# A fused two-layer block on one core: 64 instead of 48 tokens take their expert up rows by gather, and the tensor engine's up rounds are written out

## What is computed

```
q = (xt @ w_query).reshape(T, PEER_HEADS, 2, PEER_HALF)
scores = einsum('thpc,hpnc->thpn', q, sub_keys);  top 16 of each half, top 16 of the 256 sums
experts = i1 * 128 + i2            # 8 heads x 16 = 128 experts of 16384 for each token
u = take(expert_down, experts);    hdn = gelu(einsum('ted,td->te', u, x))
vsel = take(expert_up, experts);   y = einsum('te,ted->td', gates * hdn, vsel)
```

## Time and profile before

| | us |
|---|---|
| median of 3 runs (3017.72 to 3021.58) | 3018.91 |
| the profiled execution, its own time | 3036.75 |
| its span, first to last instruction | 3034.7 |
| PE busy in the span | 2999.1 (99%) |
| DVE busy | 1970.3 (65%) |
| ACT busy | 1473.1 (49%) |
| POOL busy | 945.9 (31%) |

### The profile page before, as it was taken

The page is one execution under the profiler, slowest core; times in us unless marked ns, Lnnn a source line. Parts: engine busy times, 40 slices in busy tenths (PEclk is TensorE's granted clock), DMA queues, the critical chain, the costliest instruction groups (busy, mean ns, idle before and its releaser), DMA issues.

```text
span 3034.7 us, 44598 instructions
## 1 busy us (share of the span) xinstructions
PE 2999.1 (99%) x16703; PEld 2676.0 (88%) x16703; DVE 1970.3 (65%) x2549; ACT 1473.1 (49%) x1794; POOL 945.9 (31%) x675
## 2 busy tenths in 40 slices
PE   9999999999999999999999999999999999999998
PEld 8999888888888888998999999999878888888887
DVE  5445564688875555687988976645776555555554
ACT  6445454555564444544444444554555434444443
POOL 3110000088888887155777840000000000000000
PEclk9999999999999999999999999999999999999999
DMA  7764467577777778898999985654446666666664
GB/s 228 246 205 140 147 216 253 187 210 204 213 204 203 225 209 260 296 334 308 351 363 351 349 308 193 191 180 136 132 146 187 192 191 193 191 191 193 190 193 153
DMA packets 227280, 672.30 MB, mean 222 GB/s; under 512 B 57116, under 2 KB 60838, under 8 KB 226737
## 3 DMA queue, kind: packets, MB, share of 16 engines
q1 hardware_dynamic: 157696, 549.79, 55.5%
q0 software_dynamic: 63680, 103.36, 11.8%
q10 hardware_dynamic: 5744, 16.99, 1.5%
HBM read 631.85 MB, written 38.12 MB: 221 GB/s over the span
## 4 chain that ended last, share of the span: by engine, by line
PE 95%; DVE 2%; issue 1%; ACT 1%; DMA 1%; ACTq 0%; SPq 0%; DVEq 0%
PE ps L1954 14%; PE ps L2248 10%; PE ps L2095 8%; PE ps L2097 8%; PE ps L2096 8%; PE ps L1933 8%; PE ps L1934 8%; PE ps L1932 8%; PE ps L1953 7%; PE ps L2247 5%; PE ps L1950 1%; PE ps L2261 1%; PE ps L2260 1%; PE ps L2262 1%; DVE w_lo L691 1%
## 5 line engine op out<-in xcount | busy, mean ns | idle before, releaser
L691 DVE TENSOR_TENSOR w_lo<-raw,w_hi 128x1024 fp32r<-128x1024 f32 (+2 forms) x1072 | 1274.0, 1194 | 855.7 <-ACT w_hi L686 801.1
L686 ACT ACTIVATE w_hi<-raw 128x1024 fp32r<-128x1024 f32 (+2 forms) x1072 | 1107.4, 1034 | 1274.0 <-PE ps L1934 338.4
L1954 PE MATMUL ps<-x_all,w_hi 128*128 128x512 f32 x1920 | 667.7, 390 | 0.0
L1953 PE MATMUL ps<-x_all,w_lo 128*128 128x256 f32 x1920 | 541.7, 282 | 2.3 <-DVE w_lo L691 2.3
L551 POOL DMA_INDIRECT gates<-srch x256 | 486.4, 1900 | 160.5 <-issue 78.5
L2248 PE MATMUL ps<-acts,w_hi 128*128 128x416 f32 x1680 | 514.4, 370 | 3.7 <-issue 3.7
L2247 PE MATMUL ps<-acts,w_lo 128*128 128x208 f32 x1680 | 437.7, 261 | 5.3 <-issue 4.9
L2095 PE MATMUL ps<-w_hi,x_all 128*128 128x440 f32 (+2 forms) x1152 | 436.4, 379 | 0.4 <-DVE w_lo L691 0.4
L1954 PEld LDWEIGHTS ps<-x_all,w_hi 128*128 128x128 f32 x1920 | 360.5, 188 | 74.6
L2096 PE MATMUL ps<-w_lo,x_all 128*128 128x440 f32 (+2 forms) x1152 | 424.7, 369 | 0.0
L2097 PE MATMUL ps<-w_hi,x_all 128*128 128x440 f32 (+2 forms) x1152 | 424.7, 369 | 0.0
(11 more groups left out here) (390 smaller groups left out, 3522.4 us busy)
## 6 DMA issues: line engine op xcount, KB each, us to landing
raw<-in_peer_down SPq DMA_DIRECT2D x256, 512.0 KB
raw<-in_peer_up SPq DMA_DIRECT2D x256, 512.0 KB
raw<-in_w_mlp_in SPq DMA_DIRECT2D x128, 512.0 KB
raw<-in_w_mlp_out SPq DMA_DIRECT2D x128, 512.0 KB
raw<-in_w_in SPq DMA_DIRECT2D x112, 440.0 KB
raw<-in_w_in SPq DMA_DIRECT2D x96, 428.0 KB
raw<-in_w_out SPq DMA_DIRECT2D x64, 512.0 KB
gates<-zero POOLq DMA_DIRECT2D x32, 512.0 KB, 4.9
```

Source lines behind the costliest of these rows:

```text
L686: act.activation(w_hi[:, c % RING, 0:2 * n], raw[:, c % RING, 0:2 * n], ACT.Copy).then_inc(hi_made, 1)
L691: nc.vector.tensor_tensor(w_lo[:, c % RING, 0:2 * n], raw[:, c % RING, 0:2 * n], w_hi[:, c % RING, 0:2 * n].bitcast(F32), ALU.subtract).th ...
L1953: mm(o[:, 0], wl, xh, start=False, stop=False)
L1954: last = mm(o, wh, both, start=False, stop=(k == KT - 1))
```

## The change

```diff
-WAVES = ((32, P - 32, 0), (16, P - 32 - 16, 32))
-SETS = 32 + 16
+WAVES = ((32, P - 32, 0), (32, P - 32 - 32, 32))
+SETS = 32 + 32
 TD = S - SETS
...
 SET_AT = [14 + s * 212 // SETS for s in range(SETS)]
-SETS_BY = (3, 7, 15, 22, 29, 36, 44, 48)
+SETS_BY = (3, 8, 18, 28, 37, 47, 57, 64)
...
-            up(0)
-            with pe.Fori(1, PEER_ROUNDS - 1) as r:
+            for r in range(PEER_ROUNDS - 1):
                 up(r)
```

## The result

The changed kernel takes **3099.03 us** (median of 4 runs, 3093.29 to 3103.26) beside 3020.24 us for the kernel before, run on the same chip (3017.72 to 3024.10). The ratio is 1.0262, 95% interval 1.025 to 1.0275: slower by 79 us. The forecast was 3071 in a range of 3030 to 3112. The direction and the bound were right; the size was about 28 us short in the profiled execution (3099.43 us, span 3097.6).

What follows compares the result with a forecast made beforehand. POOL's gathers were to bound the up rounds, 88 us each instead of 77. The profiled 3036.75 us, plus 36.0 for the later end of up round 6, less 1.8 for packing, gave 3071 us, range 3030 to 3112.

Steps and rivals of the forecast that it cites:

- The bound: Up rounds: POOL's back-to-back gathers become the bound, DVE and then PE wait for it; a round 88 us instead of 77.
- The products: PE's up blocks: the wide product of each pair shrinks by 0.0133 us, a block becomes 18.44 us, 28 blocks save 24 us.
- the floor: PE's last round: a short product costs 0.112 us whatever its width, so narrower products save nothing there.
- The gathers: POOL in up rounds: 48.3 gathers a round at 1.70 us each; up round 6 ends 36.0 us later in the profiled execution.
- The line through 1.52 at 76% and 1.85 at 89.5%: POOL's gather price in us against DVE's busy share, slope 2.4; it gave 1.70 us a gather.
- The start: POOL's round-long run of gathers, begun at 1353.19 before, was to begin at 1349.3 with PE's faster blocks.
- packing: Second pack on ACT: eight small transfers fewer, -1.8 us (bounds 0 and -2.3).
- two stalls: PE's stalls of 10.95 and 8.55 us in the profiled execution before, together 19.5 us, read as belonging to that execution.
- Writing out: PE's up rounds without the loop: between 0 and 11 us a round for instruction fetching, taken as 0 behind POOL.
- PE stays the bound: Rival, up rounds: gathers get quicker as soon as DVE waits, below 1.40 us for full effect; 2993 us, chance 0.11.
- Memory bounds: Rival, up rounds: 29.7 MB a round takes 79 us and POOL does not bound; about 3024 us, chance 0.09.
- No quicker than now: Rival, POOL: a gather stays at 1.85 us, 42 us more than the sum; 3113 us, chance 0.12 of more than 3112.

Runs made afterwards that it cites:

- e3: The changed kernel without the gather of one hidden activation a token and set (64 of the 320 gathers): 3043.47 us, ratio 1.0087 to the kernel before.
- e5: The changed kernel with DVE's weighted row sums over 512 of the 2048 columns, every gather kept: 3042.58 us, ratio 1.0077 to the kernel before.
- e4: The changed kernel with each row gather fetching 256 of its 512 columns, as many gathers: 3101.20 us, ratio 1.0287 to the kernel before.
- e10: The changed kernel without hidden gathers, with half of each row's bytes and row sums over 512 columns: 2993.12 us, ratio 0.991 to the kernel before.
- e13: The changed kernel with each row sum of 2048 columns written as four instructions of 512, nothing left out: 3121.41 us, ratio 1.0334 to the kernel before.
- e8: The kernel before with the products on 192 tokens, but still 48 sets gathered and PE's loop kept: 3008.60 us, ratio 0.9971.
- e6: The changed kernel without hidden gathers and with half the bytes of each row gather: 3040.01 us, ratio 1.0077 to the kernel before.
- e7: The changed kernel with the eight loads a round of hidden values and gates issued by SyncE instead of GpSimd from the second up round: 3084.56 us, ratio 1.0223.
- e2: The changed kernel with PE's loop over up rounds put back, 64 sets kept: 3096.22 us, ratio 1.0265 to the kernel before.
- e1: The kernel before with only PE's up rounds written out, 48 sets kept: 3027.57 us, ratio 1.0042.
- e12: The kernel before with products on 192 tokens, 48 sets gathered, and PE's up rounds written out: 3015.45 us, ratio 0.9988.

## Why the prediction was right, and where its size failed

**The bound: right.** Back-to-back gathers, POOL's idle time before L576 gone, DVE waiting at L1505 and PE behind it, blocks of 23.0 us on average from round 2: as written. Only the transfers were slower than the 330 to 345 GB/s named there (323 to 332 in windows of a round). e3 and e5 show the bound from both sides (fewer gathers, cheaper gathers: each 56 us back), e4 shuts memory out, and e10 shows that PE runs at its own pace once gathers are fewer and cheaper.

**The products: 18.44 us a block in the sum, 18.38 measured.** Round 0 took 73.5 us, four blocks of 64 pairs, and e10 has four rounds of 73.5. A pair went from 0.3015 to 0.287 us, so it lost 0.014 where the sum had 0.0133. The last round's triples stayed at 0.112 us each (97.9 us for the round both times), so the floor that the earlier trace rows suggested holds there. It cost nothing in the end, as POOL bounds.

**The gathers: the term that was mis-sized.** From the first gather behind round 2's loads, the sum said 1349.3 + 280 x 1.70 + 30.5 = 1855.8. Measured: 1359.10 + 280 x 1.765 + 30.5 = 1883.8; the last gather, of L566, ends at 1883.74. Of the 28 us, 18.2 are the price and 9.8 the start.
- *The price.* The line through 1.52 at 76% and 1.85 at 89.5% of DVE treated it as a function of DVE's share. The share alone doesn't fix it. Near 79% it is 1.62 us in e10, 1.765 in the change and 1.88 in e13; near 89% it is 1.75 in e3, 1.77 in e8 and 1.91 in e6. (e5 has 1.55 at 71%, e7 1.82 at 83%.) What counts is how long the operations are that a gather meets and how they are strung together. From the sum of L squared / 2 one would have got T = 48.3 x (1.25 + 53 / T) + 6.1, T = 94 us, nearer the measured 91.8 than my 88.2, though this was found only afterwards, and the same estimate misses e3 and e8 by 0.15 and 0.10 us.
- *The start.* I let the run begin as early as PE's faster blocks allow. But POOL was late already in round 1. Its 20 row gathers from 1266 to 1350 take 45.2 us, 2.26 each (line view of that stretch), with four of 5.1 us:

```profile
1344.43 5.09 POOL L560 DMA_INDIRECT big<-in_peer_up,big  x1 [0.30 <-issue]
1349.83 1.70 POOL L560 DMA_INDIRECT big<-in_peer_up,big  x1 [0.30 <-issue]
```

  The kernel before has none that long in this stretch. Four times (5.1 - 1.4) is 15 us, more than the 9.8. Round 1 also issues a fifth set (`SETS_BY` goes from 3 to 8, where it went from 3 to 7), which the sum left out, but POOL had 16 us of idle time there to take it. e5 shows it: with the fifth set and no gather over 3 us its run begins where the sum put it,

```profile
1349.25 1.01 POOL L560 DMA_INDIRECT big<-in_peer_up,big  x1 [0.30 <-issue]
```

  The gather of 1344.43 started while the row sum of 1343.22 to 1345.56 ran and ended 0.82 us after 1348.70, when two splits and a product of activations had passed too. This is e13's long wait, in the change itself.

The rest of the sum held: the up rounds start 1.7 us earlier (forecast for packing -1.8; PE's 2.3 us of waits before are gone), and the last round and the tail are unchanged within 2 us. Against the profiled execution of before: 66.3 us in up rounds 0 to 6, -1.7 and -1.7 make the 62.9 between the spans; against the medians it is 79, as that execution had its two stalls. (Its page has 308 GB/s in the two slices with the stalls, not the 334 given ahead as the lowest.)

**Writing out: nearly right.** Taken at 0 behind POOL: e2 confirms it. Its full size without POOL's bound, for which the prediction had 0 to 11 us a round, was 9.5 us in all (e1) and 6.9 (e12). The Trainium skill (Runtime: NRT & Kernel Launch, "Instruction fetch mechanics") gives stalls at taken branches as a reason to prefer full unrolling; no run here gained from it.

**The rivals.** "PE stays the bound" was refused for the right reason, though a sentence of the Trainium skill speaks for it (SBUF — State Buffer, "Who interferes with whom": the inference that descriptor writing isn't held up by `tensor_tensor`). It doesn't hold for these gathers: they end 0.82 us after a `tensor_tensor` of two SBUF operands, as the rows at 1504.03 and 1506.30 show. The same section says, for DVE's 2-port modes, that whoever issues first has the shared ports for the whole instruction; gathers that end 0.82 us behind the end of the whole operation agree with that, but the gathers of 5.1 us, which outlast the operation that they met, do not. "Memory bounds" is refuted for this kernel by e4. Whether memory would be next stays open: e3 ran at a DMA share of 0.98 and 367 GB/s with POOL idle at times, and e6 with half the row bytes was no faster, but there the gathers had become dearer. A run with neither hidden gathers nor long adds and with whole rows would tell; it wasn't tried. "No quicker than now" had only 0.12, but its 3113 us lie 14 from the measured time and the forecast's 3071 lie 28; the price was 1.765, between 1.70 and 1.85. PE's granted clock is 0.91 to 0.94 in the windows of a round. From 1353 to 1890 it fell nine times to 0.5, that is 1.2 GHz, for 3 to 14 us each: seven times during a wait of PE of 5 to 11 us, and twice just behind a wait of 1.7 to 1.8 us. I read these dips as hidden, since PE would otherwise wait for POOL; no run tests that.

No version with the whole output beat the kernel before. The products alone bring 10 us, and gathering sixteen more tokens costs 12 gathers a round, 21 us at the measured price, for which POOL had 6.5 us of idle time (25.9 in four rounds).

## What to carry to other kernels

An engine that shows 84% busy (POOL, 78.76 of 94 us) can be the bound when its instructions are spaced by an issue gap: count its instructions a round, times duration and gap, and look for idle time that is left in front of its waits. The price of such an instruction may depend on another engine: estimate it as its bare time plus what it meets of that engine's operations (here right to 0.15 us of 1.75), solve for the round length, and expect part of every saving to be taken back as the round gets shorter (e6, e7). Before cutting long operations of the other engine into short ones, run it: here it made single gathers of 3 to 6 us frequent (22 where there were none).

## What was not expected of the hardware

- Indirect DMAs on GpSimd end 0.82 us after the end of a VectorE operation with two SBUF operands that was running when they started, but take 0.95 us beside one that adds from PSUM and one SBUF operand (all seven such gathers of the change's up rounds 0 to 6).
- They can miss several gaps in a row: up to 6.17 us for one, 22 of 230 over 3 us in e13, none of 245 in the change's same stretch, 4 of 202 in that of the kernel before.
- The writing out of 3072 products cost 7 to 10 us in all where POOL didn't bound. In the profiles it lies in more and longer waits of PE for the splits (3.5 us against 0.3, 16.0 against 10.9).
